# The scan's decay rows, cumulative sums and group products ahead of the latent heads, the latent transposes in the scan, and one gate by transfers

## The reference

```
def ssd_chunked(xh, dt, A, Bm, Cm):                # the scan: 16 heads in 2 groups
    xdt   = xh * dt
    a_cum = cumsum(dt * A)
    Lmat  = exp(where(causal, a_cum[l] - a_cum[s], -inf))   # decay, one matrix a head
    cb    = einsum('bclgn,bcsgn->bclsg', Cc, Bc)            # group products, one a group
    y     = einsum('bclsg,bclsgr,bcsgrp->bclgrp', cb, Lmat, xdt) + ...   # the carried state
def hybrid_mixer(h, ...):
    z, xs, Bm, Cm, dt_raw, cq, ckv, k_rope = split(h @ w_in)
    y     = ssd_chunked(...) + d_skip * xs
    y_ssd = rmsnorm(y * silu(z), by group)
    attn  = mla_causal_attention(q, k, v)                   # 8 latent heads, 96 wide, values 128 wide
    y_mla = rmsnorm(attn)
    return concatenate([y_ssd, y_mla]) @ w_out
x = x + g2 * hybrid_mixer(...)        # g2: 1024 numbers, computed from c by w_ada
x = x + 0.5 * g3 * swiglu(...)        # ffn2
```

## Time and profile before

| | us |
|---|---|
| median of 3 runs | 1203.23 |
| profiled execution | 1203.99 |
| its span | 1202.4 |
| PE busy | 1170.0 |
| DVE busy | 866.6 |
| ACT busy | 617.4 |
| POOL busy | 73.5 |

### The profile page before, as it was taken

One profiled execution on the slowest core, in us unless ns is written; L12 is line 12 of the kernel. 1 busy time (PEld: TensorE's weight loads), 2 busy tenths in 40 slices (PEclk: granted clock), 3 DMA queues, 4 the chain that ended last, 5 costly groups with the idle time before them and its releaser, 6 DMA issues.

```text
span 1202.4 us, 18597 instructions
## 1 busy us (share of the span) xinstructions
PE 1170.0 (97%) x7211; PEld 1036.0 (86%) x7211; DVE 866.6 (72%) x1243; ACT 617.4 (51%) x827; POOL 73.5 (6%) x112
## 2 busy tenths in 40 slices
PE   8999999999999999999999999999999999999997
PEld 8897899999888789999978888888988888888886
DVE  6687798888867769888566765657986876655655
ACT  5545544444545554444466444446756756545443
POOL 9200011110000001110000000000000000000000
PEclk9999999999999999999999999999999999999999
DMA  7733698998364259998545656544651053655560
GB/s 252 228 115 112 211 365 305 327 303 290 121 198 132 78 210 338 316 309 295 188 127 176 205 181 205 167 160 159 192 187 60 15 200 123 211 188 187 171 218 35
DMA packets 143238, 236.33 MB, mean 197 GB/s; under 512 B 6357, under 2 KB 106950, under 8 KB 143174
## 3 DMA queue, kind: packets, MB, share of 16 engines
q1 hardware_dynamic: 130402, 196.73, 49.1%
q0 software_dynamic: 10400, 37.77, 8.7%
q10 hardware_dynamic: 2372, 0.96, 0.3%
HBM read 234.37 MB, written 1.05 MB: 196 GB/s over the span
## 4 chain that ended last, share of the span: by engine, by line
PE 90%; DVE 5%; ACT 3%; issue 1%; POOL 0%; ACTq 0%; DVEq 0%; POOLq 0%
PE ps L2248 10%; PE ps L1997 10%; PE ps L1999 10%; PE ps L2001 10%; PE ps L1887 7%; PE ps L1889 7%; PE ps L1888 7%; PE ps L2251 5%; PE ps L1934 2%; PE ps L1936 2%; PE ps L1935 2%; PE ps L2086 1%; PE ps L2087 1%; PE ps L2088 1%; PE ps L2021 1%
## 5 line engine op out<-in xcount | busy, mean ns | idle before, releaser
L1093 DVE TENSOR_TENSOR wlo<-raw,whi 128x2048 fp32r<-128x2048 f32 (+2 forms) x185 | 417.1, 2259 | 174.3 <-ACT whi L623 173.9
L623 ACT ACTIVATE whi<-raw 128x2048 fp32r<-128x2048 f32 (+2 forms) x185 | 348.5, 1888 | 210.5 <-PE ps L2001 111.9
L1887 PE MATMUL ps<-a,whi 128*128 128x256 f32 x720 | 204.1, 283 | 2.5 <-DVE wlo L1586 1.5
L1888 PE MATMUL ps<-a,whi 128*128 128x256 f32 x720 | 203.7, 283 | 0.0
L1889 PE MATMUL ps<-a,wlo 128*128 128x256 f32 x720 | 203.7, 283 | 0.0
L2248 PE MATMUL ps<-a,whi 128*128 128x512 f32 x576 | 143.9, 392 | 1.4 <-DVE wlo L1093 1.4
L1887 PEld LDWEIGHTS ps<-a,whi 128*128 128x128 f32 x720 | 138.0, 192 | 4.4 <-DVE wlo L1586 1.8
L1888 PEld LDWEIGHTS ps<-a,whi 128*128 128x128 f32 x720 | 138.0, 192 | 1.2
L1889 PEld LDWEIGHTS ps<-a,wlo 128*128 128x128 f32 x720 | 138.0, 192 | 0.0
L2248 PEld LDWEIGHTS ps<-a,whi 128*128 128x128 f32 x576 | 104.6, 189 | 21.2 <-issue 1.8
L1997 PE MATMUL ps<-whi,hh 128*128 128x512 f32 x376 | 116.7, 391 | 0.0
(11 more groups left out here) (424 smaller groups left out, 1926.1 us busy)
## 6 DMA issues: line engine op xcount, KB each, us to landing
stage<-in_w_ada_dram POOLq DMA_DIRECT2D x72, 512.0 KB, 6.7
raw<-in_w_up_dram SPq DMA_DIRECT2D x32, 1024.0 KB, 7.1
raw<-in_w_down_dram SPq DMA_DIRECT2D x32, 1024.0 KB, 7.7
raw<-in_ffn_w_gate_dram SPq DMA_DIRECT2D x22, 1024.0 KB, 5.3
raw<-in_ffn_w_up_dram SPq DMA_DIRECT2D x22, 1024.0 KB, 5.4
raw<-in_ffn_w_down_dram SPq DMA_DIRECT2D x22, 1024.0 KB, 5.1
raw<-in_moba_w_qkv_dram SPq DMA_DIRECT2D x11, 1024.0 KB, 6.4
raw<-in_w_in_dram SPq DMA_DIRECT2D x10, 1024.0 KB, 5.2
```

What stands on the lines that cost most here:

```text
L623: A.activation(whi[:, s, 0:size], raw[:, s, 0:size], ACT.Copy).then_inc(w_hi, 1)
L1093: V.tensor_tensor(wlo[:, s, 0:size], raw[:, s, 0:size], whi[:, s, 0:size].bitcast(F32), ALU.subtract).then_inc(w_lo, 1)
L1887: T.matmul(o, wmh, xh[:, c], start=(c == 0), stop=False)
L1888: T.matmul(o, wmh, xl[:, c], start=False, stop=False)
```

## The change

It touches only the mixer and the gate g2.

- The row form of the cumulative sums and the two group products are computed behind `heads_T(qtok)` and ahead of z's third quarter, into banks 6 and 7; the form with tokens on partitions is computed ahead of the first latent score, into free columns of bank 2. DVE copies and splits the rows straight from PSUM (no `rowf`, no ACT step) and copies the group products to `cb`, which now lies in `nB`. PE's first transpose and first product of the latent heads wait for these copies.
- Behind the latent heads only z's last quarter is left ahead of the decay rows. DVE makes the scan's first product ahead of its scaling of the latent rows, ACT scales its tile behind head 1's exponentials.
- The latent output's transposes stand behind the products of scan head 2, and its high and low parts behind heads 4 to 7.
- The gate g2 is no longer broadcast on PE: POOL writes its 1024 numbers from `modT` to device memory and later reads the row back into `g1` (which lies in `hh`) on all partitions.

```diff
+        g1 = hh[:, 0:2].rearrange("p k c n -> p (k c n)").bitcast(F32)
-        cb = st[:, 8192:8192 + 2 * SEG].rearrange("p (g n) -> p g n", g=2)
+        cb = nB[:, 0:2 * SEG].rearrange("p (g n) -> p g n", g=2)
-        mix_diag = st[:, 10240:11264].rearrange("p (c n) -> p c n", c=CT)
+        gate_row = nc.dram_tensor("gate_row", (D,), F32, kind="Internal").ap()
...
             pool.wait_ge(pv_done, 2 * H)
             fetch_part(ADA0, ADA1)
+            pool.wait_ge(a_out, 1)
+            pool.dma_start(gate_row.rearrange("(c p) -> p c", p=P), modT[:, 1, 2 * CT:3 * CT],
+                           allow_slow_non_contiguous=True).then_inc(gate_out, 16)
+            pool.wait_ge(gate_out, 16)
+            pool.wait_ge(w_used, U_TAIL)
+            pool.dma_start(g1, bass.AP(gate_row.tensor, 0, [[0, P], [1, D]])).then_inc(gate_landed, 16)
...
-            act.wait_ge(row_f, 2)
-            A.activation(rowc[0:H], rowf[0:H], ACT.Copy).then_inc(crow_hi, 1)
-            act.wait_ge(r_ready, 3)
-            A.activation(xn[:, 1], xn[:, 1], ACT.Copy, scale=newt[:, 2, 1:2]).then_inc(mla_act, 1)
-
             act.wait_ge(ac_done, 1)
             for h in range(H):
                 act.wait_ge(row_ps, h + 1)
...
-                if 1 <= h <= 4:
-                    gained("mla", bh, col(vA, COL_A, "mla_norm_w_2"), first=h - 1, npairs=h, bank_of=MLA_BANK)
+                if h == 1:
+                    act.wait_ge(r_ready, 3)
+                    A.activation(xn[:, 1], xn[:, 1], ACT.Copy, scale=newt[:, 2, 1:2]).then_inc(mla_act, 1)
+                if 4 <= h <= 7:
+                    gained("mla", bh, col(vA, COL_A, "mla_norm_w_2"), first=h - 4, npairs=h - 3, bank_of=MLA_BANK)
...
-                    if h == 3:
-                        gate_diag(1, mix_diag)
...
+                    row = g1 if b == PART["ffn2"] else gB
+                    link(V.tensor_tensor(xn[:, t, cols], row[:, cols], bank(2 * t + v), ALU.mult))
...
             link(ins)
+            dve.wait_ge(row_ready, 1)
+            dve.wait_ge(cb_ps, 1)
+            V.tensor_copy(rowc[0:H, 0:S], ps[0:H, 6, 0:S])
+            V.tensor_copy(rowc[0:H, S:SEG], ps[0:H, 6, P:S]).then_inc(row_hi, 1)
+            for gr in range(2):
+                V.tensor_copy(cb[:, gr, 0:S], ps[:, 7 - gr, S * gr:S * gr + S])
+            ins = V.tensor_copy(cb[:, :, S:SEG], ps[:, 7, S:2 * S].rearrange("p (g n) -> p g n", g=2))
+            ins.then_inc(cb_done, 1)
+            dve.wait_ge(row_hi, 1)
+            V.tensor_tensor(rowc[32:32 + H, 0:S], ps[0:H, 6, 0:S], rowc[0:H, 0:S].bitcast(F32), ALU.subtract)
+            V.tensor_tensor(rowc[32:32 + H, S:SEG], ps[0:H, 6, P:S], rowc[0:H, S:SEG].bitcast(F32),
+                            ALU.subtract).then_inc(crow_done, 1)
             splits(U_OUT)
+            dve.wait_ge(ac_ps, 1)
+            V.tensor_scalar(sm[:, 7], ps[:, 2, SEG:SEG + TT * H], -1.0, None, ALU.mult).then_inc(ac_done, 1)
             mla_heads(2 * H, QK ** -0.5)
...
+            decay(0)
             V.tensor_scalar(xn[:, 0], xn[:, 0], r[:, 0:1], None, ALU.mult).then_inc(mla_done, 1)
-            rows_lo(1)
-            dve.wait_ge(cb_ps, 1)
-            for gr in range(2):
-                ins = V.tensor_copy(cb[:, gr], bank(gr, SEG))
-            ins.then_inc(cb_done, 1)
+            decay(1)
...
-            gate_copy(1, 1.0)
...
             heads_T(qtok)
+            pe.wait_ge(ssd_in, 1)
+            pe.wait_ge(z_done, 1)
+            a = sm[:, 6].rearrange("p (t h) -> p t h", t=TT)
+            T.matmul(ps[0:H, 6, 0:S], a[:, 0], cum[:, 0:S], start=True, stop=False)
+            T.matmul(ps[0:H, 6, P:S], a[:, 1], cum[:, 0:P], start=False, stop=True).then_inc(row_ready, 1)
...
             mla_heads(2 * H)
...
             pe.wait_ge(o_ready, 4)
             z_part(3, 1, bank(4), True, True).then_inc(w_used, 1)
-            gate_rows(1, (5, 6), mix_diag)
-            pe.wait_ge(crow_done, 1)
-            pe.wait_ge(cb_done, 1)
             pe.wait_ge(sel_done, 1)
+            pe.wait_ge(exped, 2 * H + HM)
...
-            pe.wait_ge(row_f, 2)
-            pe.wait_ge(z_raw, 2)
-            transposes(xn, [(mla_done, 1), (mla_act, 1)], MLA_BANK)
             pe.wait_ge(xdt_done, 1)
+            pe.wait_ge(o_ready, 6)
...
+                if h == 2:
+                    pe.wait_ge(z_raw, 2)
+                    transposes(xn, [(mla_done, 1), (mla_act, 1)], MLA_BANK)
```

More of the change, by code:

```diff
@@ L302, in build @@
         crow_ps = sem("crow_ps")
+        row_ready = sem("row_ready")
+        row_hi = sem("row_hi")
         row_f = sem("row_f")
@@ L1812, in add_half @@
                 return V.tensor_tensor(xs[:, t, cols], xs[:, t, cols], z[:, t, cols], ALU.mult)
-            for h in range(H):
-                dve.wait_ge(dec_exp, h + 1)
-                if h >= 2:
-                    dve.wait_ge(y_done, h - 1)
-                V.tensor_tensor(pb[:, h % 2], tb[:, h % 2], cb[:, h // CT], ALU.mult).then_inc(dec_m, 1)
-                if 1 <= h <= 4:
-                    gained("mla", bh, bl, gcol("mla_norm_w_2"), first=h - 1, npairs=h, bank_of=MLA_BANK)
+            for h in range(2, H):
+                decay(h)
+                if 4 <= h <= 7:
+                    gained("mla", bh, bl, gcol("mla_norm_w_2"), first=h - 4, npairs=h - 3, bank_of=MLA_BANK)
                 if h in (10, 12):
@@ L2457, in _ @@
             heads_T(qtok)
+            pe.wait_ge(ssd_in, 1)
[3 more added lines that the diff above has]
+            T.matmul(ps[0:H, 6, P:S], a[:, 1], cum[:, 0:P], start=False, stop=True).then_inc(row_ready, 1)
+            pe.wait_ge(conv_out, 6)
+            for gr in range(2):
+                b_g, c_g = bc[:, gr], bc[:, 2 + gr]
+                T.matmul(ps[:, 6 + 1 - gr, S * gr:S * gr + S], b_g[:, 0:P], c_g, start=True, stop=True)
+                ins = T.matmul(ps[:, 7, S + P * gr:SEG + P * gr], b_g[:, P:S], c_g[:, P:S], start=True, stop=True)
+            ins.then_inc(cb_ps, 1)
             pe.wait_ge(conv_acc, 6)
@@ L2462, in _ @@
             pe.wait_ge(mqk_copied, 1)
+            T.matmul(ps[:, 2, SEG:SEG + H], cum[:, 0:P], a[:, 0], start=True, stop=True)
+            T.matmul(ps[:, 2, SEG + H:SEG + 2 * H], cum[:, P:S], a[:, 0], start=True, stop=False)
+            T.matmul(ps[:, 2, SEG + H:SEG + 2 * H], cum[:, 0:P], a[:, 1], start=False, stop=True).then_inc(ac_ps, 1)
             for h in range(2):
@@ L2508, in _ @@
                 half, hc = divmod(h, 8)
-                if h == 0:
-                    pe.wait_ge(gate_done, 2)
-                elif hc == 0:
+                if h and hc == 0:
                     pe.wait_ge(in_ready, PAIR0["mla"] + 2)
```

42 lines of the change are left out of this document (16 added, 26 removed).

## The result

The changed kernel took 1205.74 us in the median of 12 runs (1204.04 to 1207.09), the kernel before 1203.65 us in the runs beside them (12, 1203.06 to 1203.96): ratio 1.0017, 95% interval 1.0009 to 1.0024. That is no change by the 0.2% of the prediction, but the time lies above the predicted range (1201.5 to 1205.6) and 2.1 us above the forecast of 1203.6.

The account below looks back on a forecast made before the run. PE bounds the kernel, busy 1170.0 of 1202.4 us. The terms 2.75 - 0.27 - 4.0 + 1.66 + 0.2 give +0.34 us on the median of 1203.23, so 1203.6 us; range 1201.5 to 1205.6.

Parts of the forecast that it names:

- Sums and group products, +2.75: Nine matmuls moved ahead of the latent heads, where PE is full, make every latent head 2.75 us later.
- the gate diagonal, -0.27: One DVE instruction gone ahead of latent head 4's maximum: 0.27 us less, bounds 0 and -1.13.
- rival B: Latent heads or z work take in the 2.75 us of work moved ahead: 1200.8 us, chance 0.08.
- Start of the scan, -4.0: From the last latent product to scan head 0: 5.8 us for 9.8, bounds -3.0 and -4.3.
- Rival E: ScalarE's exponential or squares run a microsecond behind at the scan's start, gain 3.0 for 4.0: 1204.6 us, chance 0.08.
- Transposes, +1.66: The latent output's transposes return inside the scan behind the third head, costing 1.66 us; matmuls behind them wait for nothing.
- waits in the scan, +0.2: Waits at scan heads taking latent operands come to 1.4 to 1.8 us for 1.38; bounds -1.4 and +2.2.
- A: The 1.38 us of waits in the scan's first heads go and don't come back: 1202.0 us, chance 0.16.
- D: Scan's circle of row, exponential, operand and product closes, 1.9 us a head over four heads, +2.2: 1205.8 us, chance 0.12.
- Gate by transfers, nothing: POOL's write and spread of the gate row cost nothing, hidden by the mixer; a spread takes 5.7 us.
- Rival C: POOL's transfer blocks DVE ahead of the first feed-forward network, up to 4.2 us: 1207.8 us, chance 0.03.
- three signs of being wrong: Latent heads under 2 us later; scan heads 4 to 8 at 1.0 or 1.9 us each; anything before 900 us moved.

Follow-up runs that it names:

- fill_z2: Changed kernel with four unread PE transposes in the 0.44 us wait ahead of z's last quarter; 1204.27 us, ratio 1.0012.
- gate_only: Kernel before with only the gate sent by transfers, no broadcast on PE and no copy on DVE; 1203.54 us, ratio 0.9996.
- fill14: Changed kernel with 14 unread PE transposes in the 1.56 us wait ahead of scan head 0; 1204.06 us, ratio 1.0002.
- fill_hz: Changed kernel with both earlier waits filled by unread PE transposes (eight and four), the 1.56 us wait left; 1205.51 us, ratio 1.0014.
- trans_first: Changed kernel with the latent output's transposes ahead of scan head 0 again; 1207.51 us, ratio 1.0030.
- fill_h: Changed kernel with eight unread PE transposes in the wait ahead of the last latent head's transposes; 1206.55 us, ratio 1.0017.
- rows_first2: Changed kernel with the decay rows of heads 0 and 1 ahead of z's last quarter; 1207.02 us, ratio 1.0028.
- v1: Kernel before with the gate by transfers, group products in PSUM banks 6 and 5, DVE's copies behind the latent rows' scaling; 1202.50 us, ratio 0.9988.
- v2: v1 with the three small token-form sums moved into the wait ahead of the last latent head's transposes; 1202.22 and 1202.39 us, ratios 0.9995 and 0.9996.
- long_fill2: long_wait with 20 unread PE transposes in its 2.28 us wait; 1204.14 us, ratio 1.0009.
- long_wait: gate_only plus one DVE instruction on a scratch row ahead of the latent norm, making PE's wait 2.28 us; 1204.89 us, ratio 1.0037.

## Why the prediction was wrong

The median was missed by 2.14 us. Of these 0.42 are the kernel before, whose median is 1203.65 over 12 runs where three gave 1203.23. The undropped runs of the changed kernel lie 0.49 above it (1204.14 to 1203.65), forecast 0.37: 0.12. The other 1.60 (1205.74 to 1204.14) are the clock.

The traces can be laid over each other from the query transposes (902.99 us before, 902.95 in fill_z2, whose clock never fell) to the output matrix (956.33 and 956.59): 53.34 and 53.64 us, +0.30 where the sum had +0.34. By its steps:

- *Sums and group products, +2.75, and the gate diagonal, -0.27: right.* Counted from the query transposes (902.67 in the changed kernel's trace) the last latent product comes 2.6 us later, forecast 2.5; rival B is out. The matmuls take 2.08 us ahead of z and 0.58 ahead of the first latent score. What the diagonal gave shows only in gate_only: there the last latent head's transposes come 0.34 us sooner (926.48 for 926.82). DVE had 4.96 us to do from 904 to 910 for 3.40, and nothing of it stuck out.
- *Start of the scan, -4.0: right in its times.* From the last latent product to head 0 it takes 5.8 us (931.0 to 936.76), forecast 5.8. The two waits are 0.6 and 1.7 us by starts, forecast 0.6 and 1.65, both released by what the prediction named. Rival E is out.
- *Transposes, +1.66, and waits in the scan, +0.2: right.* In fill_z2's trace, at full clock, the first decay row to the output matrix takes 21.85 us (934.74 to 956.59), forecast 22.0. The waits (0.33, 0.18, 0.18, 0.62) are those of the kernel before, and this line:
```profile
944.69 0.44 PE L2494 MATMUL ps<-rowc,selr 128*128 128x384 f32 x1 [0.18 <-DVE work L1818]
```
The first three stand three heads later, the last where it stood. From head 0 to the output matrix it takes 19.54 us where it took 17.81, so that the waits grew by under 0.1; the 0.35 us at heads 1 and 2 didn't come. Rivals A and D are out. That D's 1205.8 lies next to the measured 1205.74 is chance: its circle of 1.9 us a head stands nowhere; heads 5 to 7 take 1.51, 1.35 and 1.35 us in that trace, as heads 2 to 4 did before.
- *Gate by transfers, nothing: right.* POOL was busy 0.93 us with the write of 1024 single numbers (the row is below), and it landed after 10.3 us; the second transfer landed in 4.1, forecast 5.7. DVE was busy 28.92 us from 600 to 640 where it was 28.93, PE 38.09 for 38.08. Rival C is out. The Trainium skill ("SBUF — State Buffer", "Who interferes with whom") lets DVE and GpSimd block each other on a shared port pair; as in the trace before, no row here shows it.
```profile
L617 POOL DMA_DIRECT2D gate_row<-modT x1: 934/934/934, 613.3 to 613.3; - x1
```
- *The step that failed:* "A wait that comes in (PE idle from 932.85 to 934.5) is the price of PE being ahead", costed at its length and nothing more, and the check "the change takes 2.14 us away and gives nearly all of it back as waits". Work replaced by waiting was taken as neutral. It isn't: the wait was where and as long as forecast, and behind it PE ran at half clock in 9 of 12 runs, for 6.8 us in the changed kernel's trace and 3.4 in that of the middle group. fill14 shows it, with the same instructions, the same waits of the other engines, and PE busy instead of idle. The forecast took the clock of 1.00 in every stretch of the earlier trace rows over to a kernel that no longer does what these rows show. Its list of what could go wrong had none on PE's clock, so the upper end of the range lay 0.14 us too low. None of its three signs of being wrong came, although the time was: they asked for the heads' places and lengths, and these were right.
- *Small slips that carry nothing:* 928.25 and 1.02 make 929.27, not 929.33; the same wait is 1.65 us in one place and 1.67 in the check; and D's +2.2 comes on top of the +0.2, so that the bound named after it should be +2.4.

The Trainium skill ("TensorE: Matmul & The Clock Gate", "Part 1: The HAM clock gate") describes the two levels, and that the clock follows how busy PE has been; the traces agree on the levels (1.00 and 0.50), and fill14 (0 of 11 dropped for 9 of 12) on what moves it. The same page's section "Why this matters for your kernels" warns of idle gaps between bursts. The gaps that dropped the clock here, 1.56 us in 5 and 6 of 11 runs, are shorter than those it warns of, so here the measurement decides.

## What to carry to other kernels

Where PE is the bound, moving its work out of a stretch that waits for a chain of other engines gains nothing if the chain's end stays where it is, and it can cost: here the work had kept the clock up. After such an edit read the granted clock in steps of 1 or 2 us behind each new wait, and take a dozen run times, since one profile shows one of the groups. If the wait can't go, a few unread transposes in it are a cheap test of whether the clock is the cause, and in the changed kernel also the cure (0 of 22 runs dropped).

## What the runs showed of the hardware

- With the same program and the same waits the clock fell in some runs and not in others: 9 of 12 for waits of 0.44 and 1.56 us, 5 and 6 of 11 for 1.56 alone, 6 of 12 for 2.28 in another place, 8 of 8 for 2.15 and 7 of 7 for 3.09 ahead of head 0, but 0 of 11 for 1.69 ahead of the decay rows and 0 of 11 for 0.9 ahead of head 0.
- In the traces the clock was at half for 3.4 us (fill_hz, trans_first), 6.8 us (changed, fill_h, rows_first2) or 23.7 us (v1). In the changed kernel and its fillings the dropped runs take 1.2 to 1.7 or 2.4 to 3.0 us more than the others, and none lies between.
- The long one costs more and varies: 9.6 us in v1's trace, 9 to 10 in one run each of v2 (twice) and long_fill2, 7.5 to 11.4 in 5 of the 12 runs of long_wait. Up to the scan's end the longest wait is 0.94 us in v1 and long_fill2 and 0.62 in v2. What starts it isn't settled.
- The clock fell only after PE had taken up work again: 0.2 us after it in trans_first, 1.1 in fill_h, 1.4 in the changed kernel, 1.5 in rows_first2 and 1.8 in fill_hz. So the slow instructions can stand well behind the wait that belongs to them.
